# End of the down products by tiles, input chain by tiles, low parts of 128-column chunks on VectorE

## The reference

```python
def gated_post_add(x, y, g_post, gate, weight):            # first block, sublayers s0 to s6
    return x + weight * gate[:, None, :] * rms_norm(y, g_post)
def modulate_pre(x, g_pre, shift, scale):
    return rms_norm(x, g_pre) * (1.0 + scale[:, None, :]) + shift[:, None, :]
def swiglu_ffn(h, w_in, w_out):                            # 1024 -> 2 x 2816 -> 1024
    g, u = jnp.split(h @ w_in, 2, axis=-1)
    return (jax.nn.silu(g) * u) @ w_out
...
        x = x + g1 * y                                      # second block, s7 to s10: no norm of y
        x = x + g2 * swiglu(modulate(rmsnorm(x, norm2_g[i]), sh2, sc2), ffn_w_gu[i], ffn_w_down[i])
```

## Time and profile before

| what | us |
|---|---|
| runs | 2491.8, 2496.27, 2498.62 |
| median | 2496.27 |
| profiled execution, span | 2491.7 (34745 instructions); its own time outside the span isn't given |
| TensorE products busy | 2244.0 (90%) |
| TensorE weight load busy | 1875.3 (75%) |
| VectorE busy | 1202.0 (48%) |
| ScalarE busy | 959.1 (38%) |
| loads of one unit of ffn_w_in, issue to landing | 6.4 (median) |
| loads of one unit of ffn_w_out | 4.9 (median) |

### The profile page before, as it was taken

One profiled execution on the slowest core, in us unless ns is written; L12 is line 12 of the kernel. 1 busy time (PEld: TensorE's weight loads), 2 busy tenths in 40 slices (PEclk: granted clock), 3 DMA queues, 4 the chain that ended last, 5 costly groups with the idle time before them and its releaser, 6 DMA issues.

```text
span 2491.7 us, 34745 instructions
## 1 busy us (share of the span) xinstructions
PE 2244.0 (90%) x14158; PEld 1875.3 (75%) x14158; DVE 1202.0 (48%) x1921; ACT 959.1 (38%) x1416; POOL 14.6 (1%) x45
## 2 busy tenths in 40 slices
PE   4899897999879998777999799878999999898998
PEld 1798686898778987434897699656777768786997
DVE  0444555444624445555444565684422232665454
ACT  0433423333533335444433544464222122455333
POOL 1000000000000000000000000000000000000000
PEclk9999998999969999778999899999999999899999
DMA  7776486776437773102776522102444242222553
GB/s 284 273 277 253 169 301 222 254 255 260 163 133 256 254 262 126 51 1 85 248 259 253 127 85 85 35 1 85 153 165 155 87 167 101 76 85 77 187 176 118
DMA packets 243800, 411.37 MB, mean 165 GB/s; under 512 B 8157, under 2 KB 188854, under 8 KB 243670
## 3 DMA queue, kind: packets, MB, share of 16 engines
q1 hardware_dynamic: 243190, 408.49, 46.7%
q0 software_dynamic: 480, 1.05, 0.6%
HBM read 408.47 MB, written 1.05 MB: 164 GB/s over the span
## 4 chain that ended last, share of the span: by engine, by line
PE 76%; DVE 10%; ACT 7%; DMA 4%; issue 2%; SPq 0%; DVEq 0%; ACTq 0%
PE bank L1422 18%; PE bank L1352 13%; PE bank L1354 13%; PE bank L1353 13%; PE bank L1330 4%; PE bank L1441 2%; PE bank L1442 2%; PE bank L1443 2%; DMA stage<-in_ffn_w_out 2%; ACT gate_b L689 1%; DMA ada<-in_ada_w 1%; ACT w_hi L555 1%; PE bank L1531 1%; PE bank L1473 1%; DVE h_lo L956 1%
## 5 line engine op out<-in xcount | busy, mean ns | idle before, releaser
L879 DVE TENSOR_TENSOR w_lo<-stage,w_hi 128x2048 fp32r<-128x2048 f32 x255 | 584.4, 2292 | 763.4 <-ACT w_hi L555 763.4
L555 ACT CAST w_hi<-stage 128x2048 fp32r<-128x2048 f32 x255 | 485.3, 1903 | 748.3 <-PE bank L1422 287.2
L1352 PE MATMUL bank<-h_hi,w_hi 128*128 128x256 f32 (+1 forms) x2432 | 736.0, 303 | 1.2 <-DVE h_lo L956 1.2
L1353 PE MATMUL bank<-h_lo,w_hi 128*128 128x256 f32 (+1 forms) x2432 | 726.5, 299 | 0.0
L1354 PE MATMUL bank<-h_hi,w_lo 128*128 128x256 f32 (+1 forms) x2432 | 726.3, 299 | 0.0
L1352 PEld LDWEIGHTS bank<-h_hi,w_hi 128*128 128x128 f32 x2432 | 466.2, 192 | 62.5 <-issue 45.6
L1353 PEld LDWEIGHTS bank<-h_lo,w_hi 128*128 128x128 f32 x2432 | 466.1, 192 | 14.7 <-issue 1.2
L1354 PEld LDWEIGHTS bank<-h_hi,w_lo 128*128 128x128 f32 x2432 | 465.9, 192 | 13.8
L1422 PE MATMUL bank<-w_hi,h_hi 128*128 128x512 f32 x776 | 242.8, 394 | 13.8 <-DVE h_lo L888 11.7
L1422 PE MATMUL bank<-w_hi,h_lo 128*128 128x512 f32 x776 | 240.8, 392 | 0.0
L1422 PE MATMUL bank<-w_lo,h_hi 128*128 128x512 f32 x776 | 240.4, 391 | 0.0
(11 more groups left out here) (192 smaller groups left out, 2007.4 us busy)
## 6 DMA issues: line engine op xcount, KB each, us to landing
ada<-in_ada_w SPq DMA_DIRECT2D x120, 1024.0 KB, 7.0
stage<-in_ffn_w_in SPq DMA_DIRECT2D x88, 1024.0 KB, 6.4
stage<-in_ffn_w_out SPq DMA_DIRECT2D x44, 1024.0 KB, 4.9
stage<-in_ffn_w_gu SPq DMA_DIRECT2D x44, 1024.0 KB, 5.1
stage<-in_ffn_w_down SPq DMA_DIRECT2D x22, 1024.0 KB, 4.9
stage<-in_a_w_in SPq DMA_DIRECT2D x12, 1024.0 KB, 7.8
stage<-in_diff_w_in SPq DMA_DIRECT2D x12, 1024.0 KB, 5.1
ada<-in_kv_ada_w SPq DMA_DIRECT2D x8, 1024.0 KB, 8.3
```

The lines of the kernel that those rows point to most:

```text
L555: a.copy(w_hi[:, s, :], stage[:, s, :]).then_inc(hi_done, 1)
L879: v.tensor_tensor(w_lo[:, s, :], stage[:, s, :], w_hi[:, s, :].bitcast(F32), ALU.subtract).then_inc(lo_done, 1)
L1352: m.matmul(dst[:, 0:T], wh, h_hi[:, k * T:(k + 1) * T], start=(k == 0), stop=False)
L1353: m.matmul(dst[:, 0:T], wh, h_lo[:, k * T:(k + 1) * T], start=False, stop=False)
```

## The change

The operations stay the same in kind; their order, their widths and the engine of one half of the normalising change.

- `down`: the last three units go tile by tile (tile 0 takes units nb-3, nb-2, nb-1, then tile 1, ...) instead of the last one. In the last tile's last unit the left 512 columns are finished before the right ones.
- `after` and `turn`: TensorE's eight transposes of next-input tile tt-1 are put ahead of tile tt's last unit, for the last tile between its two halves. The last tile's follow behind the product. The context tiles of s7 go ahead of tile 0's last unit.
- `boundary` on ScalarE and VectorE takes the place of `between` and `prep`: for each tile the update of x in two halves (`y_update`), the sums in halves, the normalised row half on VectorE, half on ScalarE (`x_norm`), and with T=256 at once the eight chunks of 128 columns: affine op, cast, low part (`affines`, `hi`, `lo`). With T=512 two tiles are taken together (`affine_pairs`), the first pair without its low parts until the last tile's update is issued.
- Units nu and nu+1 of the next sublayer are split in `boundary`: nu behind the tile before the last (tile 0 with T=256), nu+1 at its end.
- The input of s4 is made inside s3, 128 columns by 128, in its first two units; s3 and s4 no longer have a boundary. For that the inputs of s4, s5 and s6 lie elsewhere in `h_hi` (`hb`).
- The first ada product of a sublayer comes behind the first half of its first unit. The two tiles of the result are stored separately.

The core of the diff (VectorE first, then ScalarE, then TensorE):

```diff
+            def y_update(s, tt):
+                tag, T = f"s{s['n']}", s["Td"]
+                dve.wait_ge(act_s, t.at((tag, "gateb", T // 256 - 1, 1)))
+                for h in range(2):
+                    if s["post"]:
+                        dve.wait_ge(act_s, t.at((tag, "ss", tt, h)))
+                    else:
+                        wait_y(dve, s, tag, tt, h)
+                    g = gate_b[:, tt // 2, h * 512:(h + 1) * 512]
+                    if tt:
+                        dve.wait_ge(dve_s, t.at((tag, "x", tt - 1, h)))
+                    t.done(v.tensor_tensor(upd(h), y_bank(T, tt, h)[:, :], g, ALU.mult), dve_s, (tag, "upd", tt, h))
+                    if s["post"] and h == 0:
+                        mean(0, tt, (tag, "ss", tt, 0), (tag, "mean0", tt))
+                if s["post"]:
+                    inverse(0, tt, (tag, "root", tt), (tag, "yrstd", tt))
+                for h in range(2):
+                    x = xs[:, tt, h * 512:(h + 1) * 512]
+                    dve.wait_ge(dve_s, t.at((tag, "upd", tt, h)))
+                    if s["post"]:
+                        t.done(v.scalar_tensor_tensor(out=x, in0=upd(h), scalar=st(0, tt, 4), in1=x, op0=ALU.mult, op1=ALU.add),
+                               dve_s, (tag, "x", tt, h))
+                    else:
+                        t.done(v.tensor_tensor(x, upd(h), x, ALU.add), dve_s, (tag, "x", tt, h))
+            def x_norm(s, tt):
+                tag = f"s{s['n']}"
+                mean(1, tt, (tag, "xss", tt, 0), (tag, "xmean0", tt))
+                inverse(1, tt, (tag, "xroot", tt), (tag, "rstd", tt))
+                t.done(v.tensor_scalar(xn(tt)[:, 0:512], xs[:, tt, 0:512], st(1, tt, 4), None, ALU.mult), dve_s, (tag, "xn", tt))
...
+            def affines(s, tt, src_tag):
+                for n, k in enumerate(s["ks"]):
+                    affine(s, k, tt, src_tag)
+                    if n >= 2:
+                        lo(s, s["ks"][n - 2], tt)
+                for k in s["ks"][6:]:
+                    lo(s, k, tt)
```

```diff
+            def boundary(prev, s):
+                n_prev = prev["Td"] // P if prev and prev["bsteps"] else 0
+                tiles = range(s["T"] // P) if s else range(n_prev)
+                nu = s["u"] if s else None
+                for tt in tiles:
+                    if tt >= n_prev:
+                        x_norm(s, tt)
+                if s and not n_prev and s["T"] == 256:
+                    for tt in tiles:
+                        affines(s, tt, f"s{s['n']}")
+                if s and not n_prev and s["T"] == 512:
+                    affine_pairs(s, s["ks"], s["cs"][0])
+                for tt in range(n_prev):
+                    y_update(prev, tt)
+                    if s and s["T"] == 512 and tt == n_prev - 1:
+                        lo_pairs(s, s["ks"], s["cs"][0])
+                    if s and tt in tiles:
+                        x_norm(s, tt)
+                    if s and s["T"] == 256 and tt in tiles:
+                        affines(s, tt, f"s{s['n']}")
+                    if s and s["T"] == 512:
+                        if n_prev == 2 and tt == 0:
+                            affine_pairs(s, s["ks"], s["cs"][0], False)
+                        if n_prev == 4 and tt in (1, 2):
+                            affine_pairs(s, s["ks"][4 * tt - 4:4 * tt], s["cs"][0], False)
+                    if s and tt == n_prev - 2:
+                        split(nu)
+                if s and s["T"] == 512:
+                    affine_pairs(s, s["ks"], s["cs"][1])
+                if s and n_prev:
+                    split(nu + 1)
```

```diff
                 for n in range(6):
                     split(u + n + AHEAD)
+                    if n < 2 and s["n"] + 1 < len(subs):
+                        affines(subs[s["n"] + 1], n, tag)
...
-                for_b(dve, s, lambda j, i: (split(s["u"] + s["units"] + j + AHEAD, i, RING),
+                for_b(dve, s, lambda j, i: (split(s["u"] + s["units"] + j + AHEAD, i, RING) if (i is not None or j + AHEAD < s["bsteps"]) else None,
                                             mid_split(s, j + 1, i) if (i is not None or j + 1 < s["bsteps"]) else None))
-            between(subs[-1], None)
```

```diff
+                    y_stats(prev, tt)
+                    if s and s["T"] == 512 and tt == n_prev - 1:
+                        act.wait_ge(w_used, nu)
+                        for k in s["ks"][5 if n_prev == 2 else 0:]:
+                            hi_pair(s, k, s["cs"][0])
+                    if s and tt in tiles:
+                        x_norm(prev, s, tt)
+                    if s and s["T"] == 256 and tt in tiles:
+                        for k in s["ks"]:
+                            hi(s, k, tt)
+                    if s and tt == n_prev - 2:
+                        if s["T"] == 512 and n_prev == 2:
+                            for k in s["ks"][0:5]:
+                                hi_pair(s, k, s["cs"][0])
+                        split(nu)
+                if s and s["T"] == 512 and n_prev:
+                    for k in s["ks"]:
+                        hi_pair(s, k, s["cs"][1])
+                if s and n_prev:
+                    split(nu + 1)
```

```diff
+            def turn(s, tt):
+                tag = f"s{s['n']}"
+                for h in range(2):
+                    pe.wait_ge(*((act_s, t.at((tag, "xnb", tt))) if h else (dve_s, t.at((tag, "xn", tt)))))
+                    for k in range(4 * h, 4 * h + 4):
+                        ins = m.transpose(xt(tt, k), xn(tt)[:, k * P:(k + 1) * P], ident[:, :])
+                    t.done(ins, pe_s, (tag, "tr", tt, h))
...
+                            step(j - 1, i)
+                for tt in range(n_tiles):
+                    for j in range(nb - 3, nb):
+                        if tt == 0:
+                            ready(j)
+                        if tt == n_tiles - 1 and j == nb - 1:
+                            products(j, None, tt, (0, 1), ((0,),))
+                            after(tt)
+                            ins = products(j, None, tt, (0, 1), ((1,),))
+                        else:
+                            if j == nb - 1:
+                                after(tt)
+                            ins = products(j, None, tt)
+                        if tt == n_tiles - 1:
+                            ins.then_inc(w_used, 1)
```

```diff
+            def cols_product(s, dst, slot, q, first=False):
+                T, ks = s["T"], s["ks"]
+                if first and T == 512:
+                    pe.wait_ge(dve_s, t.at((f"s{s['n']}", "h32", ks[3], s["cs"][1])))
+                for k in ks:
+                    if first:
+                        pe.wait_ge(dve_s, t.at(lo_mark(s, k)))
...
+                def after(tt):
+                    if nxt is None:
+                        return
+                    if tt:
+                        turn(nxt, tt - 1)
+                    elif nxt["T"] // P > n_tiles:
+                        for k in range(n_tiles, nxt["T"] // P):
+                            turn(nxt, k)
+                down(s, tag, s["v"] + 4 if early and s["nvec"] else None, after)
+                if nxt:
+                    turn(nxt, n_tiles - 1)
     return t
```

More of the change, by code:

```diff
@@ L277, in tiles, with out_bank @@
                 return 2 if not w.diff and n < 4 else 4
+            def out_bank(w, n, half):
+                return bank[6 if not w.diff and n == 0 else 2 * (n % 2) + half]
             def nat(w, n):
@@ L719, in wide_act @@
                         nt = w.tiles(n)
[L720 to L722 removed]
+                        halves = (1, 0) if w.diff and n == 0 else range(nt // 2)
+                        for half in halves:
+                            act.wait_ge(*unit_part(s, tag, n, half == halves[-1]))
+                            b = w.out_bank(n, half)[:, :]
                             if n < w.nk:
@@ L1555, in wide_pe @@
                         nt = w.tiles(n)
-                        for tt in range(nt):
+                        order = (2, 3, 0, 1) if w.diff and n == 0 else range(nt)
+                        if n == 1 and not w.diff:
+                            pe.wait_ge(dve_s, t.at(lo_mark(s, s["ks"][-1], s["cs"][1])))
+                        for tt in order:
                             half = tt // 2
@@ L1648, in _ @@
                     pe.wait_ge(ada_col, 3)
-                prep(s, tag)
+                    for tt in range(2):
+                        turn(s, tt)
                 u, c, T = s["u"], s["c"], s["T"]
```

398 lines of the change are left out of this document (206 added, 192 removed).

## The result

The kernel after takes 2533.15 us (median of four runs, 2530.42 to 2540.31), the kernel before 2494.34 (four runs, 2491.8 to 2498.62). The ratio is 1.0157, with a 95% interval of 1.0137 to 1.0177: slower by 39 us. The forecast was 2530, from a median of 2496.3 for the kernel before. The profiled execution of the kernel after has a span of 2529.1 us, against 2491.7.

What follows compares the result with a forecast made beforehand. The prediction took TensorE's products (90% of the span) as the bound and priced the change mainly at eleven places between sublayers. Its terms, with start and end, summed to +33.4 us, added to the 2496.3 median: 2530 us, range 2503 to 2553.

Steps and rivals of the forecast that it cites:

- Step 1: Down product's last three units: TensorE waits for unit nb-2's low activations, made after unit nb-1's low weights; cost 2.35 us.
- the clock terms: Down products slowed by low clock behind the new wait: 0.6 us put in for each, 1.6 behind s7 and s8.
- Step 2: Eight transposes move between the halves of the down product's last pass, taking 0.95 us at full clock.
- S: The moment when the down product's unit nb-4 is finished; boundary times are counted from it in us.
- Step 3: On VectorE tile 0's chunks (0.53 us a pair) and unit nu's split delay tile 1's update to S+26.1, before S+18.9.
- Step 4: Tile 1's chain from update to first affine op takes 6.2 us, before 7.8; first low part at S+33.6.
- Step 5: Next sublayer's first 24 products run at 1.2 GHz, 0.213 us each instead of 0.120; boundary +5.2 us.
- The other boundaries: Boundaries after s0 to s1, and start and end, priced singly, from -7.1 us (s6 to s7) to +6.7 (s9 to s10).
- The loads at nothing: Changed weight loads cost nothing: two units of products (11.5 us) cover a load of some 5 us.
- rival B: Weight loads come late behind the boundary: up to 3 us more at five boundaries, 2545 us; chance 0.14.
- Rival C: Tile 0's chunks finish before the last pass ends, so tile 1's update starts at S+19.8; 2488 us; chance 0.09.
- Rival D: Parts nearly cancel: pairs at 0.40 us; then the 2.35 us wait and its clock loss not paid; 2500 us; chance 0.09.

Runs made afterwards that it cites:

- e1: Kernel after, with the next unit's activations (cast and low part) put ahead of the weight split in the down product, on ScalarE and VectorE; 2498.11 us.
- e10: Kernel after, with tile 0's transposes put behind the whole last pass of the down product instead of between its halves; 2536.22 us.
- e2: Kernel after, next input T=256: ScalarE casts unit nu ahead of tile 0's high parts, VectorE makes its low part behind tile 1's normalised rows; 2514.49 us.
- e4: Kernel after, with 11 extra unread fp32 products between the down product and tile 1's transposes at boundaries with T=256 on both sides; 2519.03 us.
- e7: Kernel before, with activations ahead of the weight split and extra products, 7 behind the down product and 2 between the tiles' transposes; 2489.19 us.
- e9: Kernel after, next input T=256: tile 1's update, norm and squares put ahead of tile 0's chunks and unit nu's split; 2532.73 us.
- e3: Kernel after, with the down product's last three units unit by unit again, both tiles in each, all transposes behind them; 2543.12 us.
- e11: e5 with tile 0's transposes one half-unit earlier, ahead of tile 1's last unit; 2481.57 us.
- e5: Kernel after, with the edits of e1, e2 and e4 together, with 8 extra products instead of 11; 2482.07 us.
- e12: Kernel after, with the edits of e1 and e2 together, without extra products; 2485.39 us.
- e8: Kernel after, with s4's input chunks put behind units 2 and 3 of the key/value stage instead of units 0 and 1; 2536.30 us.

## Why the prediction was right, and by its own steps

The mechanism, the side and the size were right; the terms stand as follows. That 2530 is only 3 us off is in part luck: the change of the medians is 39 us where I had 33, and the kernel before is 2 us faster here than the median that I added the sum to.

*Step 1, the wait of 2.35 us.* Right: 2.30 to 2.36 us with two tiles, 2.84 and 2.89 with four. The waits alone make 24 us, and with the clock terms (0.6 in six stages, 1.6 in two) 31; of what e1 gives 31 came with the change. That the two agree so well is in part luck: the clock fell in five stages of ten, and at s6 other waits took the place of this one.

*Step 2, the transposes in the last pass.* Right that tile 0's chunks start from there (S+17.8 predicted; 294.12 is S+18.0). Their 0.95 us cost nothing of their own (e10).

*Step 3, the order on VectorE.* Right, and now shown by e2. The pair of 128 columns takes 0.52 us, estimated 0.53 (two ops at 0.14 saved would have made it 0.51; I had taken off 0.26). The update came at S+26.0, predicted S+26.1. The Trainium skill, "VectorE: DVE Perf Modes", section "The DRAIN you can't avoid", has the next op start when the pipe is empty, but adds that a next op which is not held starts earlier, and that sentence I had left out. This pair is 0.41 and 0.28 us long and its ops start 0.32 and 0.20 apart, so it is the added sentence that the trace agrees with, and the 14 us that I worked out by the first one had no ground.

*Step 4, the chain of tile 1.* 5.9 us from 302.14 to 308.07, predicted 6.2; the first product at S+33.3, predicted S+33.6.

*Step 5, the low clock.* Right: e4 shows it as a cost of this kernel, e7 that in the kernel before it was hidden behind the wider pairs.

*The other boundaries.* Four terms are off by 1 us or more. The largest is s2 over s3 to s4, predicted +3.2 and measured +5.7. The boundary is dearer by 1.2: the first product of s3 was 81.58 us behind s2's gate product (666.34 in the earlier trace rows less 584.76) and is 87.52 now (687.06 less 599.54), 5.9 against my 4.7, since I had counted a start behind held low parts as lost time already paid. The key/value stage costs 7.5 and not 6.7: its last but one group of products starts 151.75 us behind s2's gate product before (736.51) and 165.22 after (764.76), 13.5 in all. And s4 gives back 7.8 instead of 8.2 (159.29 less 151.53 to its gate product). The first of these is also the miss in s4 to s5 (4.7 against 5.7). s6 to s7 gave 5.9 back instead of 7.1, and s8 to s9 cost 2.7 instead of 3.7; these I did not test. At the start of s0, 16 x 0.53 less 8 x 0.79 is 2.2 and not 2.4; 2.7 was measured.

*The loads at nothing* (rival B against it). Right: the ada loads held TensorE for 20.5 us, 22.2 before, and no weight load shows among TensorE's waits. It waits for low weights once, 2.11 us at 2196.99 in s9, and that low part was held by chunk ops and casts.

*Rival C.* Its condition was forced in e9 and gives no gain, so the rival failed as a reckoning too, not only by its condition. *Rival D.* The wait of step 1 was paid in full (e1), so D was false in its second half, but for s6, where e1 has 3.5 us of other waits in its place. Its first half was false too: the pairs take 0.52 us, not 0.40.

The sum was 4.0 us short of the spans (33.4 against 37.4): 2.5 of it is s2 to s4, 1.0 is s4 to s5, and +1.2 and -1.0 at s6 to s7 and s8 to s9 nearly cancel.

What stays open: why e1 and e2 together give 6 us less than the two alone, why e10 costs 3 and not 10 us, and e3 10 and not 15 (its profiled execution, the slowest of its four, is 14.7 longer than that of the kernel after). Single steps differ by 1 to 2 us, once by 4 (e11 and e5 in s7), even where the code is the same: up to s0's gate product, where e1 and e2 have the kernel after's program, it took 223.37 us in e1 and 225.19 in e2, and between 400 and 420 us the clock was 0.83 on average in e1 and 0.74 in e12.

## What to carry to other kernels

When a pass is reordered so that an engine asks for its operands in another order, look at what is queued ahead of them on the engine that makes them: here one swap in VectorE's and ScalarE's program (e1) was worth 35 us where 39 were lost, 31 of them brought by the change, and the tile-by-tile product itself helped (e3). Splitting a chain per tile paid here once nothing long stood between the tiles' chains in program order: moving the one piece that was in the way (e2) helped, reordering a full engine's own work (e9, e8) did not. And extra work on an idle TensorE to keep its clock paid where TensorE, not its supplier, sets the pace right behind the gap (e4 against e7), and hardly at all where a new gap of 2.35 us came in between (e5).

## What the hardware showed that I had not expected

- Behind the same wait of 2.3 us the granted clock fell to 0.50 for some 3.4 us at s2, s5, s6 and s10 and stayed at 1.00 at s0, s1, s4 and s9 in the profiled execution of the kernel after; with 2.8 to 2.9 us it fell at s8 and not at s7. It is not fixed by the place either: at s0 it fell in e10 (0.50 from 281.7 to 285.1, 9 products started) and at s4 in e2 (from 967.4). The length of the wait alone does not say what it costs.
- One fp32 product of 128x512 takes 0.87 us at full clock (11 of them, recorded in two parts each, fill 9.6 us from 435.43 on in e4), where a product of the same shape in the down product, on fp32r operands, takes 0.228.
- A chunk op that reads PSUM takes 0.54 us at 256 columns and 0.40 at 128, the low part 0.41 and 0.28: half the columns cost two thirds to three quarters of the time, in ops as in pairs (0.79 and 0.52 us).
